# The last expert group's right product, made expert by expert: a decoder layer with a mixture of experts, fp32 on one core

## The reference

```python
def moe_ffn(xn, ...):
    scores = jax.nn.sigmoid(t @ w_router)            # 64 experts
    ...                                              # group-limited top 8 for each token, bias in the choice
    gates = ...                                      # 256 x 64, 8 non-zero in a row
    def add_expert(acc, params):
        wg, wu, wd, g = params                       # 1024x256, 1024x256, 256x1024
        hid = jax.nn.silu(t @ wg) * (t @ wu)
        return acc + g[:, None] * (hid @ wd), None
    routed = scan(add_expert, ...)                   # over all 64 experts
    shared = (silu(t @ w_gate_sh) * (t @ w_up_sh)) @ w_down_sh
    return routed + shared

x = x + hybrid_mixer(rms_norm(x), mem, ...)
x = x + moe_ffn(rms_norm(x), ...)
```

## Time and profile before

| | us |
|---|---|
| median of 3 runs (lowest, highest) | 585.07 (584.98, 585.52) |
| the profiled execution: device time | 585.64 |
| the profiled execution: span of its instructions | 583.9 |
| HBM read in it | 225.90 MB |
| TensorE busy | 555.0 (95%) |

### The profile page before, as it was taken

The page is one execution under the profiler, slowest core; times in us unless marked ns, Lnnn a source line. Parts: engine busy times, 40 slices in busy tenths (PEclk is TensorE's granted clock), DMA queues, the critical chain, the costliest instruction groups (busy, mean ns, idle before and its releaser), DMA issues.

```text
span 583.9 us, 8338 instructions
## 1 busy us (share of the span) xinstructions
PE 555.0 (95%) x3168; PEld 307.9 (53%) x3169; DVE 209.3 (36%) x533; ACT 159.5 (27%) x308; POOL 24.4 (4%) x78
## 2 busy tenths in 40 slices
PE   8999999999999999999999999999996999789984
PEld 6988875465544444555445444454542444345332
DVE  2788798665334322220122222222211222220113
ACT  5787366342212222220022222222220112120102
POOL 1006131000000000000000000000000000000000
PEclk9999999999999999999999999999998999898999
DMA  8997469649999999999999999999999999999995
GB/s 316 418 421 296 181 215 417 290 178 375 415 422 420 422 420 421 428 424 424 396 429 421 427 424 432 420 428 434 419 433 427 427 427 425 421 423 427 421 412 212
DMA packets 27064, 227.50 MB, mean 390 GB/s; under 512 B 3216, under 2 KB 3344, under 8 KB 7696
## 3 DMA queue, kind: packets, MB, share of 16 engines
q1 hardware_dynamic: 26736, 226.67, 93.6%
q10 hardware_dynamic: 288, 0.29, 0.1%
HBM read 225.90 MB, written 1.05 MB: 389 GB/s over the span
## 4 chain that ended last, share of the span: by engine, by line
PE 76%; DMA 9%; SPq 9%; DVE 3%; issue 1%; ACT 1%; DVEq 0%; ACTq 0%
PE ps L1775 27%; PE ps L1804 12%; PE ps L1733 8%; PE ps L1833 6%; PE ps L1640 5%; SPq L472 4%; PE ps L1536 4%; DMA cell_three<-in_w_e 3%; DMA cell_two<-in_w_e 3%; PE ps L1503 3%; SPq L590 2%; PE ps L1517 2%; SPq L584 2%; DMA cell_d<-in_w_e 2%; PE ps L1795 1%
## 5 line engine op out<-in xcount | busy, mean ns | idle before, releaser
L1775 PE MATMUL ps<-cell_two,xg 128*64 128x512 f32 (+2 forms) x528 | 117.4, 621 | 11.6 <-DMA cell_two<-in_w_e 6.4
L1804 PE MATMUL ps<-cell_d,e_hT 128*64 128x512 f32 (+2 forms) x440 | 89.7, 597 | 2.5 <-DVE e_hT L1395 2.1
L1775 PEld LDWEIGHTS ps<-cell_two,xg 128*64 128x64 f32 (+2 forms) x528 | 37.0, 131 | 85.3 <-issue 85.3
L1775 PE MATMUL ps<-cell_gu,xg 128*64 128x512 f32 (+2 forms) x416 | 78.5, 595 | 0.9 <-DMA cell_gu<-in_w_e 0.8
L1392 DVE TENSOR_TENSOR e_h<-e_sg,ps 128x256 f32<-128x256 f32 x28 | 11.8, 421 | 179.9 <-ACT e_sg L910 179.9
L910 ACT ACTIVATE e_sg<-ps 128x256 f32<-128x256 f32 x28 | 10.8, 384 | 201.6 <-PE ps L1775 201.6
L1460 DVE SCALAR_TENSOR_TENSOR ylo<-ps,gslot,yhi 128x512 fp32r<-128x512 f32 (+1 forms) x53 | 39.2, 740 | 73.5 <-ACT yhi L921 73.5
L1733 PE MATMUL ps<-pick,xhi 128*128 128x256 f32 x224 | 58.4, 299 | 0.3 <-DVE pick L1308 0.3
L921 ACT ACTIVATE yhi<-ps,gslot 128x512 fp32r<-128x512 f32 (+1 forms) x53 | 36.0, 679 | 71.3 <-PE ps L1804 69.9
L1733 PE MATMUL ps<-pick,xlo 128*128 128x256 f32 x224 | 54.3, 281 | 0.0
L1733 PEld LDWEIGHTS ps<-pick,xhi 128*128 128x128 f32 x224 | 42.2, 188 | 19.8 <-issue 19.7
(11 more groups left out here) (342 smaller groups left out, 680.4 us busy)
## 6 DMA issues: line engine op xcount, KB each, us to landing
cell_two<-in_w_e SPq DMA_DIRECT2D x33, 2048.0 KB, 23.8
cell_d<-in_w_e SPq DMA_DIRECT2D x53, 1024.0 KB, 20.7
cell_gu<-in_w_e SPq DMA_DIRECT2D x48, 1024.0 KB, 18.4
cell_three<-in_w_e SPq DMA_DIRECT2D x7, 3072.0 KB, 20.5
wo<-in_w_out SPq DMA_DIRECT2D x1, 4096.0 KB, 12.5
wA<-in_w_qk SPq DMA_DIRECT2D x7, 512.0 KB, 10.9
wR<-in_w_rest SPq DMA_DIRECT2D x3, 1024.0 KB, 28.5
wV<-in_w_v SPq DMA_DIRECT2D x1, 2048.0 KB, 18.8
```

Source lines behind the costliest of these rows:

```text
L1775: last = mm(ps[side * w:(side + 1) * w, U, :], rows(k, slice(side * w, (side + 1) * w)), weight[:, k - k0, :], start=k == 0, stop=k == KD - 1)
L1804: last = mm(ps[side * w:(side + 1) * w, Y[half], :], e_hT[:, kk, side * w:(side + 1) * w], n[:, kk, half * 512:(half + 1) * 512], start=kk ...
```

## The change

The last group's down matrices are brought in by column halves, each with both k-blocks: four transfers of left columns (512 KB each), one an expert, and then four of right columns, each with its own semaphore, `tail_loaded[n]` for expert n. TensorE makes the whole left product at once. The right product follows expert by expert: for each, a wait for its own right columns, and then both quarters with both k-blocks (`down_quarters`). Ahead of the third expert stands the left scatter with its waits. ScalarE and VectorE copy the left results (`result(0, ...)`) between the conversion of the left half and those of the quarters. To make room for the two more semaphores, the router's bias shares `rt_loaded` with the router's matrix (both engines wait for 32), and `wA_loaded[0]` goes.

```diff
-        wA_loaded = [ctx.enter_context(nc.semaphore(f"wA_loaded{n}")) for n in range(8)]
+        wA_loaded = {n: ctx.enter_context(nc.semaphore(f"wA_loaded{n}")) for n in range(1, 8)}
...
-        tail_loaded = [ctx.enter_context(nc.semaphore(f"tail_loaded{i}")) for i in range(2)]
+        tail_loaded = [ctx.enter_context(nc.semaphore(f"tail_loaded{i}")) for i in range(groups[-1].n)]
...
-            sp.dma_start(rbias[:], router_bias[0].partition_broadcast(P)).then_inc(rb_loaded, 16)
+            sp.dma_start(rbias[:], router_bias[0].partition_broadcast(P)).then_inc(rt_loaded, 16)
...
                 elif part == "down" and e in groups[-1].experts:
                     i = cell_of[part, e]
-                    sp.dma_start(cell_d[i][:, 0:1], ranked("down", chosen[e - first])[:, 0:1]).then_inc(cell_loaded[i], 16)
+                    c = slice(0, 512)
+                    sp.dma_start(cell_d[i][:, :, c], ranked("down", chosen[e - first])[:, :, c]).then_inc(cell_loaded[i], 16)
...
-            for half in range(2):
-                c = slice(half * 512, (half + 1) * 512)
-                for e in groups[-1].experts:
-                    sp.dma_start(cell_d[cell_of["down", e]][:, 1:KH, c],
-                                 ranked("down", chosen[e - first])[:, 1:KH, c]).then_inc(tail_loaded[half], 16)
+            c = slice(512, D)
+            for n, e in enumerate(groups[-1].experts):
+                sp.dma_start(cell_d[cell_of["down", e]][:, :, c], ranked("down", chosen[e - first])[:, :, c]).then_inc(tail_loaded[n], 16)
...
                     nc.scalar.mul(yhi[:, c], o, gslot[:, g.routed % 2:g.routed % 2 + 1]).then_inc(yhi_act, 1)
+                    if g is groups[-1] and i == 0:
+                        act.wait_ge(residual_ps, 1)
+                        result(0, 1)
...
             group(groups[-1])
-            act.wait_ge(residual_ps, 1)
-            for half in range(2):
-                result(half, 2 * half + 1)
+            result(1, 3)
...
-            dve.wait_ge(rb_loaded, 16)
+            dve.wait_ge(rt_loaded, 32)
...
+                    if g is groups[-1] and i == 0:
+                        dve.wait_ge(residual_ps, 1)
+                        result(0, 2)
...
             group(groups[-1])
-            dve.wait_ge(residual_ps, 1)
-            for half in range(2):
-                result(half, 2 * half + 2)
+            result(1, 4)
...
-            pe.wait_ge(rt_loaded, 16)
+            pe.wait_ge(rt_loaded, 32)
             router(0, 0)
...
-            def down_quarter(cells, kk, quarter):
+            def down_quarters(cells, side):
+
+                w = P // len(cells)
+                for c, o in results_of(groups[-1])[1:]:
+                    for kk in range(KH):
+                        last = mm(o[side * w:(side + 1) * w, :], e_hT[:, kk, side * w:(side + 1) * w], cells[side][:, kk, c],
+                                  start=kk == 0, stop=kk == KH - 1, skip_group_check=True)
+                    if side == len(cells) - 1:
+                        last.then_inc(y_ps, 1)
...
                 elif g is groups[-1]:
-                    down(cells, y_ps, (0,), range(KH - 1))
-                    for kk in range(KH - 1):
-                        for quarter in range(2):
-                            down_quarter(cells, kk, quarter)
-                    pe.wait_ge(tail_loaded[0], 16 * g.n)
-                    down(cells, y_ps, (0,), range(KH - 1, KH))
-                    pe.wait_ge(tail_loaded[1], 16 * g.n)
-                    for quarter in range(2):
-                        down_quarter(cells, KH - 1, quarter)
+                    down(cells, y_ps, (0,))
+                    for side in range(g.n):
+                        if side == 2:
+                            pe.wait_ge(S_act, NR)
+                            pe.wait_ge(yhi_act, 2 * (NR - 1) + 1)
+                            pe.wait_ge(ylo_dve, 2 * (NR - 1) + 1)
+                            scatter(S, last_ps, halves=(0,))
+                        pe.wait_ge(tail_loaded[side], 16)
+                        down_quarters(cells, side)
...
             group(groups[-1])
-            pe.wait_ge(S_act, NR)
-            pe.wait_ge(yhi_act, 2 * (NR - 1) + 1)
-            pe.wait_ge(ylo_dve, 2 * (NR - 1) + 1)
-            scatter(S, last_ps, halves=(0,))
             for quarter in range(2):
```

More of the change, by code:

```diff
@@ L329, in hybrid_decoder_layer @@
             memT_loaded, x_loaded, mem_loaded, vec_loaded, wg_loaded, wV_loaded, kv_loaded, wo_loaded, x1_loaded,
-            rt_loaded, rb_loaded, consts, zeroed, ssq_act, std_act, xn_dve, diag_dve, row_ps, row_act,
+            rt_loaded, consts, zeroed, ssq_act, std_act, xn_dve, diag_dve, row_ps, row_act,
             xT_act, xT_dve, unit_ps, unit_act, unit_dve, conv_dve, z_ps,
@@ L341, in hybrid_decoder_layer @@
         ) = [ctx.enter_context(nc.semaphore(name)) for name in """
-            memT_loaded x_loaded mem_loaded vec_loaded wg_loaded wV_loaded kv_loaded wo_loaded x1_loaded             rt_loaded rb_loaded consts zeroed ssq_act std_act xn_dve diag_dve row_ps row_act xT_act xT_dve
+            memT_loaded x_loaded mem_loaded vec_loaded wg_loaded wV_loaded kv_loaded wo_loaded x1_loaded             rt_loaded consts zeroed ssq_act std_act xn_dve diag_dve row_ps row_act xT_act xT_dve
             unit_ps unit_act unit_dve conv_dve z_ps bc_act mask_pool w_dve
```

## The result

| us | before | changed |
|---|---|---|
| median (lowest), 6 runs each | 585.09 (584.79) | 588.77 (587.3) |
| ratio, 95% interval | | 1.0048, 1.0029 to 1.0066 |
| profiled execution: device time, span | 585.64, 583.9 | 590.21, 588.5 |
| same pair again, with the experiments | 585.58 (585.06) | 587.86 (586.97), ratio 1.0044, 1.0028 to 1.0059 |

One run of the changed kernel took 950.13 us with a mean granted clock of 0.557; it counts in the median of 588.77, the ratio leaves it out, and the median of the other five is 588.27. By the ratio the changed kernel is 0.48% slower; by the median of the five it is 3.2 us, by the lowest times 2.5 us. I had forecast 1.1 us, and both medians are outside the range of 584.8 to 587.3.

The account below looks back on a forecast made before the run. The path from the last down-matrix landing to the last copy and output was taken to set the end; 0.69 (last expert's start) + 0.72 (longer path) - 0.3 (output) = +1.1 us, 586.2, range 584.8 to 587.3.

Parts of the forecast that it names:

- output behind the last copy's end, less than before's 3.06: End of the kernel: left results go out about 1.3 us earlier, gaining 0.3 us (bound 0 to 0.6).
- The step of the sum that failed: Right product on TensorE: experts overlap though issued in sequence, so experts 2 and 3 both start at 577.65.
- The price of a lone expert: Right product: one expert's eight instructions in one column group end 1.92 us after starting; costs 0.85 us for the last quarter.
- the exposed conversion of the right quarters: After the last product: yhi and ylo no longer hidden by the left scatter, 0.8 us; last copy at +3.90 against 3.18.
- The last landing: Down-matrix transfers: last right half lands at 577.25 instead of 576.96, 0.3 us later (bounds 0 and 0.4).
- 2 KB pieces: Down-matrix transfers: 42.6 us of engine time a MB against 40.3 for 4 KB pieces, 0.3 us later at each engine.
- Issue: Transfer issue on SP: 512 more pieces, 8.8 us at the very worst, under 10.4 of cover, so 0 cost.
- The start of the left scatter: TensorE, last stage: scatter starts at 576.55, behind expert 1's last instruction at 576.24, not waiting for ylo.
- The place of the left scatter: Ahead of experts 2 and 3: delays them 0.4 us; 1.13 us leave the end, 0.85 and 0.8 enter.
- right behind the left scatter and not behind a DMA wait: Profile sign: the last eight matmuls first start at 577.5 to 577.8, experts 2 and 3 together.
- 32 pairs: Profile sign: the trace would show 32 pairs of matmuls on the new quarter line of the right product.
- The *in order* rival: Right product: experts' matmuls follow each other strictly in issue order, +3.3 to +3.4 us, 588.4; 12 in 100.

Follow-up runs that it names:

- changed_again: The changed kernel, unaltered, run and profiled once more beside the kernel before: 587.86 us (lowest 586.97), ratio 1.0044.
- four_eights: Changed kernel with one wait for all right halves, left scatter mid-way, each expert's eight right-product instructions issued at once: 589.19 us, one profiled execution.
- four_blocks: Changed kernel with one wait for all right halves, right product issued four instructions of each expert at a time: 591.12 us, one profiled execution.
- pair_rounds: Changed kernel with experts 0 and 1 issued in rounds, an instruction of each in turn, and likewise 2 and 3: 587.14 us (lowest 586.20), ratio 1.0026.
- The two delay kernels: delay_before and delay_after: 2.15 us of dummy matmuls added to the kernel before (587.02 us) and to the changed kernel (590.26 us).
- eights_end: Changed kernel with left scatter and left copies back at the end, loads and expert-by-expert order kept: 587.01 us (lowest 586.1), ratio 1.0024.
- the four nestings: Changed kernel, one wait for all right halves, right product in rounds (587.7 us), as four_eights, as four_blocks, or six then two of each expert (588.04).
- delay_after: Changed kernel with five dummy matmuls (2.15 us) on TensorE ahead of the last group's transposes: 590.26 us (lowest 589.44).
- delay_before: Kernel before with five dummy matmuls (2.15 us) on TensorE ahead of the last group's transposes: 587.02 us (lowest 586.15).

## Why the prediction was wrong

Term by term, from the start of the left product, so that a late start doesn't count ("first profile" is the changed kernel's):

| from the left product's start, us | predicted | changed_again | first profile |
|---|---|---|---|
| left scatter starts | 4.45 | 4.42 | 4.43 |
| expert 2 starts | 5.55 | 5.55 | 5.55 |
| right product of experts 2 and 3 | 1.92 | 2.81 | 2.81 |
| last copy starts | 9.45 | 10.27 | 10.29 |
| output behind the last copy's end, less than before's 3.06 | 0.3 | 0.2 | 0.2 |

- **The step of the sum that failed: "an expert starts when its columns have landed and its own group is free, whether or not the expert before is done".** It is worth 0.8 us (10.27 against 9.45). Half of it was right: experts do run beside each other though issued one behind the other. (The rule of the Trainium skill, TensorE: Matmul & The Clock Gate, Part 3, section The mechanism, that matmuls start in program order, is contradicted here: four_eights would have 4 x 7 = 28 steps between its first and last start by it and has 19, and in four_blocks the thirteenth instruction started within 0.07 us of the first.) But an expert's instructions wait in a queue of four, and the memory-attention rows on which I leaned have exactly four instructions a head. They could not show the limit. With eight instructions the next expert loses 0.87 us. pair_rounds issues each pair in rounds and is 1.6 us shorter from e_hT on. The sentence on how the kernel works, that every engine's instructions run in the order of the code, holds for waits and for the order of issue, not for the starts of matmuls in different column groups.
- **The range had no term for a late start; this is the larger part.** With the queue in it the forecast would be 587.0, still inside the range; the five runs have 588.27. I wrote that the clock stood at its full level throughout, which was so in that one profile, and took the start of the stage as fixed. In the kernel before, e_hT is ready 4.9 us ahead of the last landing with 2.7 us of work to do, so that part of a delay is covered. The change puts TensorE on the path from e_hT on. The two delay kernels show the difference: 2.15 us given, 2.4 paid by the changed kernel and 1.4 by the one before. That the clock gives such delays is seen in the first profile (2.96 us in the high part), that a landing does in others (up to 1.7 us against before's). Of the timed runs only the mean clock of the whole run is known. The changed kernel's seven runs at 0.99 or more have a median of 587.74, its four at 0.984 to 0.988 have 589.27; the kernel before has 585.50 (27 runs at 0.99 or more) and 585.48 (47 below). That fits a low clock which only the changed kernel pays for, with few runs and without saying where in the run it fell. How much of each run's excess comes from the clock and how much from landings stays open.
- The price of a lone expert, 1.92 us, was right (1.91 in eights_end). So was the exposed conversion of the right quarters: +3.90 from the last expert's start, measured 3.85 (its start at 576.92 + 0.87, the copy at 581.64).
- The last landing: near, 0.2 past the 0.4 of the range. It came 12.7 us after its issue at 564.92 in changed_again, 577.6, against 577.25 predicted (576.5 in the first profile), and nothing waited for it. The right halves of experts 0, 1 and 2 landed 1.1 us earlier than predicted (572.3, 573.6 and 574.9 against 573.4, 574.7 and 576.0). In the first profile 2 KB pieces cost 43.2 us of engine time a MB where 4 KB pieces had cost 40.3 (1.052 x 16 x 1.9 us for 0.74 MB, from 565.5 to 567.4).
- Issue: right. The last issue began at 564.92 to 565.27, before before's 566.56, so the 512 more pieces cost SP nothing.
- The start of the left scatter, 4.42 against 4.45, was luck. I had expert 1 begin 0.9 us behind expert 0 because its columns landed then; they had landed at 573.6, and it was the queue that held it, 0.87 us to 573.95.
- The place of the left scatter: right, and the saving went where I said: 1.1 us leave the end, the lone expert and the bare conversion enter it. What I called "right behind the left scatter and not behind a DMA wait" is what the profile shows, for expert 2; expert 3 starts 0.87 behind it, not together with it. (The "32 pairs" of the new line are 32 instructions.)

Undisturbed, the sum with the queue in it is 1.1 + 0.8 = 1.9 us; the lowest times differ by 1.9 (586.97 against 585.06) and 2.5 (587.3 against 584.79). The rest of the 3.2 us between 588.27 and 585.09 is put down to late starts: profiled executions and the delay kernels show that they happen and that they are paid, the timed runs themselves can't be read. The *in order* rival gave 588.4, close to the measured 588.27, by a mechanism that the four nestings rule out.

## What to carry to other kernels

- When products of separate column groups are issued one behind the other, interleave them at least every four instructions (two fp32 matmuls of the source); four_blocks does and runs in the 7 steps of rounds. This was measured for fp32 and 256 columns only. A precedent in the trace proves overlap only up to its own length.
- Before work is taken from behind a landing, ask what else can be late. A stage that ends with a wait for a transfer swallows part of a slow clock or a late start; a stage that TensorE sets pays it all (3.69 us of 3.68 in delay_after's profile, 1.82 of 3.18 in delay_before's). One profile doesn't show that; a dummy delay in both kernels does.
- Splitting a wait by expert leaves one column group at work behind the last landing. Splitting it by k-block keeps all four busy (1.07 us against 1.92).

## What the runs showed of the hardware

- Matmuls of different 32-column groups start out of program order. Each group holds four instructions, the running one among them, and a full group holds up the issue to all (fp32, 256 columns): first to last start of the same 32 instructions was 4.19 us in eights, 2.89 in sixes and 1.55 in rounds (1.93 less the last one's own 0.38, as in the others).
- The stream of weight transfers ends slowly. In the kernel before the mean busy share of the 16 engines falls from 1.05 to 0.04 over 4 us, with the last landing released at 576.96. Whether some engines end early or all run thin isn't shown by the mean.
- Landings of the same bytes move from one execution to the next: two profiles of the changed kernel have the last one at 576.5 and 577.6.
- Two profiles of one program differed by 2.96 us in one product of 32 instructions, at a granted clock of 0.50 and of 1.00: TensorE had been 1.05 of 3.5 us busy ahead of it in one and 2.53 in the other.
